# Which engine adds the gathered expert rows: TensorE takes 67 of VectorE's 129

## What is computed

```
proj = rmsnorm(x) @ w_in            # qkv | z | x_lru | y_lru | gates | beta | decay
A = gated DeltaNet(q, k, v)         # 8 heads, causal conv, chunked triangular solve
B = RG-LRU(conv4(x_lru)) * gelu(y_lru)
x = x + (sigmoid(ga) * (A @ w_a) + sigmoid(gb) * (B @ w_b)) @ w_out
x = x + PEER(rmsnorm(x))            # below
y = rmsnorm(x)

PEER, for each token: q = n @ w_q; top-16 of two key halves per head, 8 heads
  -> 128 experts e with gates g
  act = gelu(peer_u[e] . n) * g     # one dot product of 1024 for each expert
  out = sum over e of act * peer_v[e]
```

## Time and profile before

| | us |
|---|---|
| median of 3 runs | 2084.38 (2083.14 to 2085.78) |
| the profiled execution, its own time | 2080.88 |
| its span in the trace | 2079.1 |

### The profile page before, as it was taken

One profiled execution on the slowest core, in us unless ns is written; L12 is line 12 of the kernel. 1 busy time (PEld: TensorE's weight loads), 2 busy tenths in 40 slices (PEclk: granted clock), 3 DMA queues, 4 the chain that ended last, 5 costly groups with the idle time before them and its releaser, 6 DMA issues.

```text
span 2079.1 us, 27628 instructions
## 1 busy us (share of the span) xinstructions
PE 1692.1 (81%) x9838; PEld 1073.1 (52%) x9838; DVE 1418.7 (68%) x3158; ACT 871.5 (42%) x2469; POOL 665.0 (32%) x549
## 2 busy tenths in 40 slices
PE   8999999889787799999897678989887656556654
PEld 7888998655454567777564445554434211111110
DVE  5063521288877588889988468897778677667764
ACT  2533222146522385547756135564413333233342
POOL 0000000124432342422444233445433544444441
PEclk9999999989999999999999888986898767766677
DMA  7344333799999999999999999999999999999997
GB/s 236 94 150 131 92 92 132 254 402 385 418 410 383 409 418 372 399 381 361 391 399 420 418 361 417 370 419 383 393 418 418 421 403 421 421 421 422 421 393 300
DMA packets 128291, 724.90 MB, mean 349 GB/s; under 512 B 16480, under 2 KB 23264, under 8 KB 58016
## 3 DMA queue, kind: packets, MB, share of 16 engines
q0 software_dynamic: 78336, 570.46, 67.4%
q1 hardware_dynamic: 49200, 150.53, 20.3%
q10 hardware_dynamic: 624, 2.23, 0.3%
HBM read 714.11 MB, written 8.52 MB: 348 GB/s over the span
## 4 chain that ended last, share of the span: by engine, by line
PE 42%; DMA 29%; DVE 19%; ACT 7%; issue 3%; POOL 1%; DVEq 0%; SPq 0%; ACTq 0%; POOLq 0%
DMA arena<-in_uv,arena 20%; PE ps L1043 8%; DVE arena L1963 7%; PE ps L1094 7%; PE ps L757 6%; PE ps L813 5%; PE ps L887 3%; DMA arena<-in_w_out 3%; PE ps L961 3%; PE ps L985 2%; DMA arena<-in_stream 2%; DMA arena<-in_w_a 2%; DVE arena L1829 1%; DVE pos L1898 1%; PE ps L905 1%
## 5 line engine op out<-in xcount | busy, mean ns | idle before, releaser
L1539 POOL DMA_INDIRECT arena<-in_uv,arena x544 | 663.8, 1220 | 1108.3 <-PE ps L1094 684.6
L1963 DVE CUSTOM_DVE_ANT_0 arena<-arena 128x1024 f32<-128x1024 f32 x544 | 659.2, 1221 | 249.0 <-DMA arena<-in_uv,arena 246.4
L1094 PE MATMUL ps<-arena 64*64 64x512 f32 (+1 forms) x3192 | 538.8, 755 | 216.9 <-ACT arena L1500 216.8
L1094 PEld LDWEIGHTS ps<-arena 64*64 64x64 f32 (+1 forms) x3192 | 114.1, 154 | 486.4 <-ACT arena L1500 365.2
L1514 ACT ACTIVATE gelu_d<-dots 128x2 f32<-128x2 f32 x272 | 55.4, 204 | 703.0 <-DVE dots L1963 702.4
L1043 PE MATMUL ps<-arena 128*128 128x294 f32 (+1 forms) x1152 | 293.2, 415 | 16.7 <-DMA arena<-in_stream 9.5
L1043 PEld LDWEIGHTS ps<-arena 128*128 128x128 f32 x1152 | 219.8, 192 | 92.7 <-issue 14.4
L961 PE MATMUL ps<-arena 128*128 128x128 f32 (+1 forms) x1024 | 139.9, 297 | 37.1 <-DMA arena<-in_w_a 21.3
L961 PEld LDWEIGHTS ps<-arena 128*128 128x128 f32 x1024 | 131.8, 202 | 61.1 <-DMA arena<-in_w_a 24.1
L757 PE MATMUL ps<-arena 128*128 128x256 f32 x640 | 143.6, 388 | 3.5 <-DVE arena L1562 3.0
L757 PEld LDWEIGHTS ps<-arena 128*128 128x128 f32 x640 | 124.4, 195 | 22.0 <-issue 3.4
(11 more groups left out here) (284 smaller groups left out, 1981.8 us busy)
## 6 DMA issues: line engine op xcount, KB each, us to landing
arena<-in_stream SPq DMA_DIRECT2D x144, 512.0 KB, 5.1
arena<-in_w_a SPq DMA_DIRECT2D x32, 512.0 KB, 10.7
arena<-in_w_out SPq DMA_DIRECT2D x32, 512.0 KB, 10.6
arena<-in_w_q SPq DMA_DIRECT2D x32, 512.0 KB, 7.7
arena<-in_uv,arena POOLq DMA_INDIRECT x544, 11.5
arena<-spill SPq DMA_DIRECT2D x2, 1920.0 KB, 13.4
arena<-in_x_prompt SPq DMA_DIRECT2D x4, 512.0 KB, 6.9
arena<-in_ln_g SPq DMA_DIRECT2D x4, 512.0 KB, 9.7
```

The source lines that it names most:

```text
L1094: mm = pe.matmul(ps[rows_out, half, :], diag[on_pe(k) % NDIAG][rows_in, 0:TS if t == NTILE else HALF_P], ring[k % SLOTS][rows_in, D + half ...
L1539: pool.indirect_dma_start(out=ring[kk % SLOTS], out_offset=None, in_=a["uv"], in_offset=bass.IndirectOffsetOnAxis(ap=idx[:, kk:kk + 1], ax ...
L1963: ins = dve.tensor_tensor_reduce(ring[s][:, 0:D], ring[s][:, 0:D], n2p if t == NTILE else n2[t % 2], 1.0, 0.0, ALU.mult, ALU.add, dots[k / ...
```

## The change

Only `on_dve` changes. Before, VectorE added 129 of the 544 rows; now it adds the 62 that lie in the projections' slots, and TensorE adds all others.

```
         def on_dve(k):
 
-            s = stage_at(k)
-            if s < BT[1] or s >= stages:
-                return False
-            if BG + LX <= s < BG + 87:
-                return s < BG + 82
-            if any(BD[u] <= s < BT[u] for u in (2, 3)):
-                return k % 8 == 3
-            tail_at = [s - b for b in BT if 0 <= s - b < 33]
-            return bool(tail_at) and (k % 2 == 1 or s >= BT[3] and KC <= tail_at[0] < 2 * KC)
+            return BG + LX <= stage_at(k) < BG + 82
```

## The result

| | before | changed |
|---|---|---|
| median | 2084.43 us (4 runs) | 2099.72 us (4 runs, 2095.67 to 2102.63) |
| profiled execution, its own time | 2080.88 us | 2099.41 us |
| span | 2079.1 us | 2097.6 us |

The ratio is 1.0054, 95% interval 1.0033 to 1.0075: the change costs 0.5%, some 11 us of the median by the ratio, 15 by the medians. The forecast was 2093 us, slower by 0.4%. The measured 2099.7 us is inside the stated range of 2075 to 2112, and the direction is the one forecast.

A forecast was written before the change was run, and what follows sets the result against it. DMA bytes at 421 GB/s were taken as the floor, so only DMA idle time counts. Terms 0 + 0 - 1 + 6 + 5 - 1 = +9 on 2080.9 give 2089.9; with 3.5 for the median, 2093 us, range 2075 to 2112.

The forecast's parts named there:

- The floor in bytes and the plateau: First gather to last: bytes set the floor, transfers reach 421 GB/s, a row costs the DMA engines 2.49 us.
- What a moved row costs: Each of 67 rows: 1.28 us off VectorE, 1.02 us onto TensorE, 1.92 at half clock; ScalarE's extra diagonal costs nothing.
- Tail 3: 20 rows move, seven between w_out products then 5.08 us long; backlog of 9.0 us nearly covers 9.7: +5, ends -1 and +11.
- the gap: Tail 3, behind the w_out products: TensorE idles 7.84 us for a diagonal; DMA engines idle for about half of it.
- Delta 3: Rows 239 to 332: 12 rows, 17.6 us on TensorE, one third not in idle time: +6, ends -3 and +17.6.
- Tail 1 and delta 2: Rows 59 to 93 and 161 to 213: 16 and 8 rows move, each 0; ends -6 and +6, -3 and +4.
- The yardstick of delta 1: Rows 13 to 58, all rows already on TensorE, run at 401 GB/s; so delta 2's engines changing places costs nothing.
- Tail 2: Rows 214 to 238: 11 rows move, TensorE has room and catching up behind the residual eases: -1, ends -5 and +2.
- Tile 2's end: Its join goes, so TensorE idles up to 2.0 us less before opening tile 3: -1, ends -2 and 0.
- In full: Rival: TensorE's added time counts fully in delta 3, tail 3 and tail 1: +35, 2119 us; chance 0.14.
- The catching up: Rival: VectorE is late behind the residual in tails 1 and 2; relieving it gains: -8.7, some 2076 us; chance 0.15.
- The clock: Rival: more rows lift TensorE to full clock in late delta 3: -4.5, 2080 us; chance 0.07.

The follow-up runs named there:

- before_again: The kernel before, unchanged, run and traced once more on the experiments' chip: 2089.16 us (one run).
- b3_rest13: Kernel before with 13 rows of tail 3, those not between the w_out products, moved to TensorE: 2090.61 us, ratio 1.0003.
- a3_tails12: Kernel before with rows 59 to 93 and 214 to 238 (tails 1 and 2) all added by TensorE, 27 moved: 2093.05 us, ratio 1.0023.
- c1_wout_all: Kernel before with VectorE also adding the even rows between the w_out products of tails 1 and 2: 2094.78 us, ratio 1.0026.
- b2_wout7: Kernel before with only rows 339 to 345, between tail 3's w_out products, moved to TensorE: 2096.35 us, ratio 1.0035.
- b1_thin7: Kernel before with all tail 3 rows on TensorE, but rows 339 to 345 added with 64 of 512 columns: 2096.70 us, ratio 1.0026.
- c3_after_wout7: Changed kernel with rows 339 to 345 of tail 3 given back to VectorE: 2097.52 us, ratio 1.0060 to the kernel before.

## Why the prediction was right, point by point

- **The floor in bytes and the plateau** held: behind the trunk both kernels move 421 GB/s, and rows 367 to 511 take 369.6 us before and 367.7 after.
- **What a moved row costs.** TensorE's 1.02 us was exact: the row of 1550.05 is followed at 1551.07, and 7 x 1.02 = 7.1 is the 7.2 us by which the products grew in each of the four traces with the rows there.
- **Tail 3** (+5, measured +6.7 and, in the changed kernel's second trace, +5.3 against before_again, on another chip). The mechanism was right to the record: products 5.08 us apart, the backlog of 15.6 us down to 8.1, a rate under 400. VectorE's wait of 13.13 us at the residual shows who stood behind TensorE. The thirteen other moved rows, which the sum had at nothing beyond the gap, cost nothing alone (b3_rest13). And the backlog lasted less far than 9.0 us promised: during the products the rate is 382 GB/s, which is 38.7 x 39/421 = 3.6 us lost, where 0.7 was taken.
- **Delta 3** (+6, read as +11.4). The term was about twice too large (2.4 by all traces, 3.6 by the changed kernel's two), and its baseline was wrong. The sum took the 255.6 us of one trace as the kernel's length. Ten traces with its rows on VectorE span 255.6 to 268.1 us, and the one that the sum was made against is the shortest. Against their mean the moved rows cost 265.0 - 262.6 = 2.4 us, with overlapping ranges; by whole runs 0.11% with an interval that holds zero. So of 17.6 us of TensorE's time about a seventh seems to have reached the path, not the third that was taken, and even that isn't settled. Of the 11.4 us that the first pair of traces shows some 5 go with the clock of the sample tile's products, for which the sum had no term.
- **Tail 1 and delta 2** (0 and 0, read +1.9 and -0.3) stayed within the 3 us. The yardstick of delta 1 held: TensorE at 91% and VectorE at 84% of delta 2 give 401 GB/s, with the two engines' shares of before (85 and 89%) the other way round.
- **Tail 2** (-1, read +2.1) has the wrong sign, but 106.5 us is within the scatter of the traces with its rows left. The gain behind the residual never came: a3_tails12 is slower, by 0.23%, with 35 us less on VectorE.
- **Tile 2's end** (-1): TensorE idles 5.59 us before it opens tile 3, near the 5.5 forecast, as this line of the changed kernel shows beside the earlier trace rows:

```profile
1687.22 1.99 PE L1078 MATMUL ps<-arena,ident 64*64 64x512 f32 x8 [5.59 <-ACT ps L1464]
```

- **The rivals.** "In full" would have been 2119 us; the thirteen free rows of tail 3 speak against it. The catching up is refuted by a3_tails12, where fewer rows on VectorE cost 0.23% instead of gaining; c1_wout_all, with more rows on VectorE there, cost something too. The clock: delta 3's mean went from 0.82 to 0.84, with TensorE busier by 14 us, so more work didn't lift it to the full level. Where its low level falls turned out to matter, 4 us and more in rows 325 to 330, though as scatter of this stretch: all 16 records were slow in four kernels that leave delta 3 alone as well.
- **The total** came near partly by luck. Against the means of the traces with rows left, the changed kernel's two traces lose 12.5 and 8.7 us in the five stretches, around the forecast's +9. But tail 3 gave 6.0 of the mean of 10.6 where 5 was taken, delta 3 3.6 for 6, and tails 1 and 2 2.0 for -1: errors of either sign that cancel. And the profiled pair, 18.5 us apart, sets the shortest delta 3 of all against nearly the longest.
- **What stays open.** By the traces tail 3 explains 6 us and the other stretches 4 to 5, most of that within their scatter; the whole runs say 11 to 15. That the seven rows cost 4 us and more is shown in the traces and by b2_wout7's whole runs, but neither b1_thin7's nor c3_after_wout7's whole runs show it given back. Of c3_after_wout7's 0.6% nothing is found in the stretches with moved rows of its one trace. More traces of one kernel would tell where its slower runs lose their time.

## What to carry to other kernels

Of two engines that can do the same work, ask at each place which of them is waited for: in the traces seven rows of 1.02 us between products that already filled TensorE cost 4 us and more, and thirteen rows on the same engine a few us away cost nothing. A queue's backlog (time from issue to landing, less the shortest) gives a first estimate of how long such an engine may be late before the transfers run dry, and here it was too kind: 9.0 us of backlog against 9.7 needed still lost 3.6. Before a stretch's length is used as a baseline, see it in a second trace: here one stretch kept to 0.1 us and its neighbour moved by 6.3.

## What the hardware showed beyond that

At the end of delta 3 TensorE was busy 22.09 of 24.50 us in the changed kernel and yet had a mean clock of 0.59. In the first 15.3 us of these it was busy without a break, and the granted clock was at its low level, 1.2 GHz, all the time; in the w_out products of tail 3 it was busy all the time too and had 1.00:

```profile
1484.70:1500.00 15.30, 15.30 (x59) 5.71 (x60) 4.60 (x11) 8.59 (x25) 1.92 (x2) 0.50 0.70 262
```

The Trainium skill (TensorE: Matmul & The Clock Gate, Part 1: The HAM clock gate) puts the low level down to an idle array; by the profile's busy time, which doesn't tell how much of the array a product uses, this row doesn't bear that out. Which of the products at the end of delta 3 goes with the low level wasn't tried. What it costs depends on where the low level falls: the same six rows of the same code took 16.2 us in one trace and up to 21.7 in others, two records of one product 0.41 and 0.63 us.
